# Two transformer blocks on one core: compression and gates with high and low parts side by side, and value stages that take the token halves in turn

## What is computed

```python
def compress(z, pe, w1, w2):
    zb = z[:, blk] + pe[None, None, :, None, :]
    zb = zb.transpose(0, 1, 3, 2, 4).reshape(b, n_cmp, NSA_KV_HEADS, CMP_LEN * HEAD_DIM)
    return jax.nn.silu(zb @ w1) @ w2
k_cmp = compress(k_c, cmp_pe[0], cmp_w1[0], cmp_w2[0])
v_cmp = compress(v_c, cmp_pe[1], cmp_w1[1], cmp_w2[1])
...
gates = jax.nn.sigmoid(gl.reshape(b, s, NSA_HEADS, 3))
```

## Time and profile before

| | |
|---|---|
| median of 3 runs | 2095.44 us (2095.3 to 2095.66) |
| the profiled execution | 2095.29 us |
| its span | 2093.5 us |
| TensorE busy | 2056.4 us, 98% |
| VectorE busy | 1482.3 us, 71% |
| ScalarE busy | 1022.6 us, 49% |
| GpSimd busy | 483.1 us, 23% |
| mean granted TensorE clock | 0.996 |
| DMA | 369.99 MB, 177 GB/s |

### The profile page before, as it was taken

How to read it: one execution, slowest core, us unless ns; L and a number is a source line. 1 busy time by engine, 2 the same in 40 slices (tenths; PEclk the granted TensorE clock), 3 DMA queues, 4 the chain that set the end, 5 groups by cost and what they waited for, 6 DMA issues and landing times.

```text
span 2093.5 us, 29532 instructions
## 1 busy us (share of the span) xinstructions
PE 2056.4 (98%) x11608; PEld 1771.4 (85%) x11608; DVE 1482.3 (71%) x2054; ACT 1022.6 (49%) x1508; POOL 483.1 (23%) x441
## 2 busy tenths in 40 slices
PE   7999999999999999999999999999999999999997
PEld 6788888888888888887878888888888888888886
DVE  8866778788776556876646668777776567777755
ACT  5445444455633554653455555554544344455443
POOL 8305553300000344340211224310110001101122
PEclk9999999999999999999999999999999999999999
DMA  7554566556654333555444445555556665655664
GB/s 249 172 185 155 178 191 194 190 184 221 218 185 149 121 109 118 181 203 186 161 150 146 143 151 181 182 191 183 191 190 181 189 191 185 191 187 186 186 186 131
DMA packets 104090, 369.99 MB, mean 177 GB/s; under 512 B 11632, under 2 KB 12944, under 8 KB 103824
## 3 DMA queue, kind: packets, MB, share of 16 engines
q1 hardware_dynamic: 103952, 368.11, 55.6%
HBM read 365.97 MB, written 2.10 MB: 176 GB/s over the span
## 4 chain that ended last, share of the span: by engine, by line
PE 94%; DVE 4%; issue 0%; ACT 0%; DMA 0%; DVEq 0%; SPq 0%; ACTq 0%
PE psg L511 51%; PE psg L513 25%; PE psg L558 2%; PE psg L560 2%; PE psg L559 2%; PE psg L510 2%; DVE s_wl L1579 2%; PE pst L511 1%; PE pst L595 1%; DVE s_rh L1597 1%; PE pst L513 1%; DVE s_ry L1597 1%; PE pss L759 1%; PE pso L779 0%; PE pst L683 0%; PE pst L684 0%
## 5 line engine op out<-in xcount | busy, mean ns | idle before, releaser
L1579 DVE TENSOR_TENSOR s_wl<-s_stage,s_wh 128x1024 fp32r<-128x1024 f32 (+3 forms) x699 | 871.5, 1247 | 374.5 <-ACT s_wh L1050 371.6
L1050 ACT ACTIVATE s_wh<-s_stage 128x1024 fp32r<-128x1024 f32 (+3 forms) x699 | 729.1, 1043 | 789.9 <-PE psg L511 429.0
L511 PE MATMUL psg<-s_ry,s_wh 128*128 128x512 f32 x2672 | 941.0, 397 | 3.3 <-DVE s_mv L1646 2.5
L513 PE MATMUL psg<-s_ry,s_wl 128*128 128x256 f32 x2501 | 706.8, 283 | 0.0
L511 PEld LDWEIGHTS psg<-s_ry,s_wh 128*128 128x128 f32 x2672 | 492.5, 188 | 111.4 <-issue 3.1
L513 PEld LDWEIGHTS psg<-s_ry,s_wl 128*128 128x128 f32 x2501 | 470.6, 188 | 7.7
L511 PE MATMUL psg<-s_rh,s_wh 128*128 128x512 f32 x1280 | 456.9, 400 | 10.9 <-DVE s_rh L1597 9.1
L513 PE MATMUL psg<-s_rh,s_wl 128*128 128x256 f32 x1180 | 334.7, 284 | 0.0
L511 PEld LDWEIGHTS psg<-s_rh,s_wh 128*128 128x128 f32 x1280 | 237.4, 189 | 61.1 <-issue 8.0
L511 PE MATMUL psg<-s_hid,s_wh 128*128 128x512 f32 x704 | 244.6, 394 | 0.0
L513 PEld LDWEIGHTS psg<-s_rh,s_wl 128*128 128x128 f32 x1180 | 223.8, 190 | 3.6
(11 more groups left out here) (390 smaller groups left out, 2280.1 us busy)
## 6 DMA issues: line engine op xcount, KB each, us to landing
...
```

The source lines that it names most:

```text
L511: m = e.matmul(o, M.WH[:, r, ws], xx, start=begin, stop=end)
L513: m = e.matmul(o[:, T:2 * T], M.WL[:, r, ws], xh, start=False, stop=False)
L1050: e.activation(M.WH[:, c % NR, 0:n], M.ST[:, c % NS, 0:n], ACT.Copy).then_inc(S["wh"], 1)
L1579: e.tensor_tensor(M.WL[:, c % NR, 0:n], M.ST[:, c % NS, 0:n], M.WH[:, c % NR, 0:n], ALU.subtract).then_inc(S["wl"], 1)
```

## The change

*Side by side.* The z parts now lie in one [128, 128] tile, high part in columns 0 to 59 and low part in 64 to 123, and `WH` and `WL` are two views of one tile `W` [128, 3, 2, 1024]. One matmul of 512 columns (256 of the high and 256 of the low part of w1) replaces three of 256; the product low x low is computed along with them. The accumulator is then a whole bank: VectorE sums its two halves (`hsum`), and a real matmul with a 0/1 matrix `stk` adds the rows of the high and the low part while it turns them over; it replaces the transposes, and tanh and silu come behind it on 128 columns. The gate's unit is stored so that its high and low 36 columns stand side by side, sixteen matmuls with 72 outputs replace sixteen pairs, and a matmul with `gstk` adds and turns over.

*Spread.* The row of units becomes

```diff
@@ -61,6 +61,8 @@
...
     put("ident", (p == f).astype(np.float32))
+    put("stk", (p % 64 == f[:, 0:64]).astype(np.float32))
+    put("gstk", ((p < 72) & (p % 36 == f[:, 0:36])).astype(np.float32))
@@ -236,7 +238,7 @@
...
         for w in range(2):
-            for _ in range(3):
+            for _ in range(3 if w == 0 else 0):
@@ -244,13 +246,13 @@
...
                 yield
-            for _ in range(4):
+                if w == 0 and m < 5:
+                    yield
+            for _ in range(6):
...
             yield
-            if w == 0:
-                yield
@@ -283,9 +285,9 @@
...
     P.group([(("kc", j), P.halves("wkv", j)) for j in range(4)])
+    P.between = P.compress()
...
         P.tile(("vc", j), P.halves("wkv", 4 + j))
-    P.between = P.compress()
@@ -345,8 +347,8 @@
...
         self.ST = fix("stage", [128, NS, UW])
-        self.WH = fix("wh", [128, NR, UW], F32R)
-        self.WL = fix("wl", [128, NR, UW], F32R)
+        self.W = fix("w", [128, NR, 2, UW], F32R)
+        self.WH, self.WL = self.W[:, :, 0, :], self.W[:, :, 1, :]
@@ -462,7 +464,25 @@
...
 
-        return self.ZB[m % 3][:, part, i, :].rearrange("p (h n) -> p h n", h=4)[:, :, 0:15]
+        return self.ZB[m % 3][:, i, 64 * part:64 * part + 64].rearrange("p (h n) -> p h n", h=4)[:, :, 0:15]
+
+    def gate_weights(self, r):
+
+        return self.W[:, r, :, :].rearrange("p s c -> p (s c)")[:, 0:KT * 72].rearrange("p (k c) -> p k c", k=KT)
+
+    def weights(self, c, part, n):
+
+        if n == KT * 36:
+            return self.gate_weights(c % NR)[:, :, 36 * part:36 * part + 36]
+        return self.W[:, c % NR, part, 0:n]
+
+    def staged(self, c, n):
+        s = self.ST[:, c % NS, 0:n]
+        return s.rearrange("p (k c) -> p k c", k=KT) if n == KT * 36 else s
+
+    def hid(self, part):
+
+        return self.HT[:, part, :, :].rearrange("p a (h n) -> p a h n", h=4)[:, :, :, 0:16]
@@ -541,15 +561,15 @@
...
         banks = [P.bank[t, i] for i in range(2)]
-        vacant(*banks)
-        for i in range(2):
-            held[banks[i]] = P.out[t, i]
+        vacant(banks[0])
...
             w.wait_ge("wl", c + 1)
-            steps = [(kk, i) for i in range(2) for kk in range(2)] if u == 7 else [(kk, i) for kk in range(2) for i in range(2)]
+            steps = [(kk, i) for i in range(2) for kk in range(2)] if u in (0, 7) else [(kk, i) for kk in range(2) for i in range(2)]
             for n, (kk, i) in enumerate(steps):
+                if u == 0 and n == 2:
+                    vacant(banks[1])
@@ -562,6 +582,8 @@
...
             unit()
+        for i in range(2):
+            held[banks[i]] = P.out[t, i]
@@ -679,22 +701,22 @@
...
                     ws = slice(i * 256, i * 256 + 256)
-                    o = M.PST[:, 0, 0:T]
-                    e.matmul(o, zb[:, 0, i, :], M.WH[:, r, ws], start=(m == 0 and i == 0), stop=False)
-                    e.matmul(o, zb[:, 0, i, :], M.WL[:, r, ws], start=False, stop=False)
-                    x = e.matmul(o, zb[:, 1, i, :], M.WH[:, r, ws], start=False, stop=(m == 7 and i == 3))
+                    x = e.matmul(M.PST[:, 0, :], zb[:, i, :], M.W[:, r, :, ws], start=(m == 0 and i == 0), stop=(m == 7 and i == 3))
...
                 yield
-            held["t", 0] = ("hcs", v + 1)
-            for _ in range(3):
+                if v == 0 and m < 5:
+                    yield
+            held["t", 0] = ("hsum", v + 1)
+            yield
+            vacant(("s", 0))
+            w.wait_ge("hsum", v + 1)
+            for k in range(2):
+                x = e.matmul(M.PSS[:, 0, 64 * k:64 * k + 64], M.ZT[v][:, 128 * k:128 * k + 128], M.con("stk", 64), start=True, stop=True)
+            x.then_inc(S["hct"], 1)
+            held["s", 0] = ("hcs", v + 1)
+            for _ in range(5):
                 yield
-            vacant(("s", 0))
-            w.wait_ge("hcs", v + 1)
-            e.transpose(M.PSS[:, 0, 0:128], M.ZT[v][:, 0:128], ident)
-            e.transpose(M.PSS[:, 0, 128:256], M.ZT[v][:, 128:256], ident).then_inc(S["hct"], 1)
-            held["s", 0] = ("htl", v + 1)
-            yield
@@ -713,16 +735,28 @@
...
             held["o", 0] = ("cmp", v + 1)
-            if v == 0:
-                yield
-                yield
+            yield
+
+    def gate_tile():
+
+        bank = P.bank["gate"]
+        vacant(bank)
+        held[bank] = P.out["gate"]
+        c = done[0]
+        r = c % NR
+        w.wait_ge("wl", c + 1)
+        for k in range(KT):
+            ready("h1")(k)
+            m = e.matmul(M.product(bank)[0:72, :], M.gate_weights(r)[:, k, :], Y(k)[1], start=(k == 0), stop=(k == KT - 1))
+        m.then_inc(S["units"], 1)
+        unit()
...
         for t in range(2):
-            m = e.transpose(M.PSO[1][:, 36 * t:36 * t + 36], M.ZT[0][0:36, t * 128:t * 128 + 128], ident[0:36, 0:36])
+            m = e.matmul(M.PSO[1][:, 36 * t:36 * t + 36], M.ZT[0][0:72, t * 128:t * 128 + 128], M.con("gstk", 36, 72), start=True, stop=True)
@@ -1047,7 +1081,7 @@
...
             w.wait_ge("units", c - NR + 1)
-        e.activation(M.WH[:, c % NR, 0:n], M.ST[:, c % NS, 0:n], ACT.Copy).then_inc(S["wh"], 1)
+        e.activation(M.weights(c, 0, n), M.staged(c, n), ACT.Copy).then_inc(S["wh"], 1)
@@ -1199,42 +1233,51 @@
...
-            w.wait_ge("units", P.end["cw1", v])
...
+            w.wait_ge("hct", v + 1)
...
-            e.activation(M.ET[v][:, :], M.PST[:, 0, 0:T], ACT.Tanh, scale=0.5).then_inc(S["hct_a"], 1)
...
-            w.wait_ge("hct", v + 1)
-            e.activation(M.HT[:, 0, :, :], M.PSS[:, 0, 0:T].rearrange("p (a b) -> p a b", a=2), ACT.Copy).then_inc(S["hth"], 1)
+            e.activation(M.ET[v][:, 0:128], M.PSS[:, 0, 0:128], ACT.Tanh, scale=0.5).then_inc(S["hct_a"], 1)
...
+            w.wait_ge("hcs", v + 1)
...
+            e.activation(M.hid(0), M.ET[v][:, 128:256].rearrange("p (a h n) -> p a h n", a=2, h=4), ACT.Copy).then_inc(S["hth"], 1)
@@ -1856,48 +1899,54 @@
...
+            w.wait_ge("units", P.end["cw1", v])
...
+            e.tensor_reduce(M.ZT[v][:, :], M.PST[:, 0, :].rearrange("p (s t) -> p t s", s=2), AX.X, ALU.add).then_inc(S["hsum"], 1)
...
-            he, bank = M.ET[v][:, :], M.PST[:, 0, 0:T]
+            he, hs = M.ET[v][:, 0:128], M.ET[v][:, 128:256]
...
-            e.tensor_tensor(M.ZT[v][:, :], bank, he, ALU.mult).then_inc(S["hcs"], 1)
+            e.tensor_tensor(hs, M.PSS[:, 0, 0:128], he, ALU.mult).then_inc(S["hcs"], 1)
...
-            e.tensor_tensor(M.HT[:, 1, :, :], M.PSS[:, 0, 0:T].rearrange("p (a b) -> p a b", a=2), M.HT[:, 0, :, :].bitcast(F32),
...
+            e.tensor_tensor(M.hid(1), hs.rearrange("p (a h n) -> p a h n", a=2, h=4), M.hid(0).bitcast(F32), ALU.subtract).then_inc(S["htl"], 1)
...
+                side.start(later(1, rope(3, M.KCMP[0:32, :, 0:15], M.COS[:, 31:256:16], M.SIN[:, 31:256:16], 4, 15, M.RTC, ("cmp", 1))))
@@ -1459,11 +1502,11 @@
...
     side.start(kv_norm())
-    nxt(5)
...
     side.start(h1_high(0, 8))
+    nxt(5)
+    side.start(compress())
     nxt(8)
-    side.start(compress())
@@ -2114,14 +2163,14 @@
...
     side.start(kv_norm())
+    side.start(h1_low(0, 8))
...
         nxt()
-    side.start(h1_low(0, 8))
+    side.start(compress())
     tiles("vc", 4, M.VC, None, 0)
-    side.start(compress())
@@ -2469,10 +2518,11 @@
...
     ticks(8)
-    ticks(8)
...
     for i in range(3):
-        e.memset(M.ZB[i][:, :, :, :].bitcast(F32), 0.0).then_inc(S["zz"], 1)
+        e.memset(M.ZB[i][:, :, :].bitcast(F32), 0.0).then_inc(S["zz"], 1)
+    e.memset(M.HT[:, :, :, :].bitcast(F32), 0.0).then_inc(S["zz"], 1)
+    ticks(8)
```

More of the change, by code:

```diff
@@ L36 @@
 _off = 0
-for _n, _w in (("ident", 128), ("cm", 128), ("ca", 32), ("c01", 32), ("ipool", 64),
+for _n, _w in (("ident", 128), ("stk", 64), ("gstk", 36), ("cm", 128), ("ca", 32), ("c01", 32), ("ipool", 64),
                ("inv", 1), ("sgn", 1)):
@@ L414, in __init__ @@
         self.VC = alloc(l1c, "vc", [128, 4, T])
-        self.ZB = [alloc(l1c, f"zb{i}", [128, 2, 4, 128], F32R) for i in range(3)]
+        self.ZB = [alloc(l1c, f"zb{i}", [128, 4, 128], F32R) for i in range(3)]
         self.HT = alloc(l1c, "ht", [128, 2, 2, 128], F32R)
@@ L670, in compress @@
         for v in range(2):
-            for _ in range(3):
+            for _ in range(3 if v == 0 else 0):
                 yield
@@ L974, in tensor_program @@
     side.start(gates())
-    tile("gate", Y, ready("h1"), (16,), 0, 36)
+    gate_tile()
     for j in range(4):
@@ L1201, in compress, with zb @@
     def compress():
-        for v in range(2):
-            def zb(m):
-                Z = (M.KC, M.VC)[v]
-                w.wait_ge("zz", 3)
-                w.wait_ge(*P.out[("kc", "vc")[v], 3])
-                if m >= 3:
-                    w.wait_ge("units", P.zb[8 * v + m - 3])
-                elif v:
-                    w.wait_ge("units", P.zb[7])
-                for i in range(4):
-                    l = 4 * m + i
```

(62 more changed lines are left out.)

33 lines of the change are left out of this document (16 added, 17 removed).

## The result

The change takes the kernel from 2095.85 us to **2088.7 us** (medians of six runs each, 2087.18 to 2090.98 after): ratio 0.9965, 95% interval 0.9956 to 0.9975. That is 7.2 us where 11.5 were forecast (2083.8). It lies inside the stated range, 0.3 us from its upper end.

The account below looks back on a forecast made before the run. PE (TensorE) was taken as the bound, busy 2056.4 of 2093.5 us, with DVE right behind in the compression's stage. Terms summed to -11.5, so 2095.3 - 11.5 = 2083.8 us; range 2080.5 to 2089.0.

Parts of the forecast that it names:

- rival A: Stage `vs` becomes bound by DVE and loads: +6.0 and more replaces +3.1, 2086.7 up to 2090; chance 0.15.
- compression, first matrix: Per compression unit, four 512-column matmuls replace twelve of 256, 1.44 us becoming 0.93; over 16 units -8.2 us.
- gate tile: Sixteen 512-column matmuls replace sixteen pairs, so sixteen matmuls of 0.120 us go: -1.9 us.
- `stk`, `gstk` for transposes: Sums over high and low rows: six real fp32 matmuls with a 0/1 matrix replace six transposes, +0.6 us.
- `vcc`, `vb`, `va`: Value stages where PE no longer waits for both accumulators, or waits less between halves: -1.3, -1.3 and -0.7 us.
- `vs`, end of the compression, new seams, DVE's lead: Wait gone at `vs` -1.1, last compression step moved inside `vw` -1.5, two new seams +0.8, DVE falling behind +3.1.
- Value stages: First accumulator takes six matmuls before the second is needed: -1.3 `vcc`, -1.3 `vb`, -1.1 `vs`; -0.7 between `va` halves.
- What the shorter units cost: Where short and long units alternate in `vs`, DVE falls back 4.4 us and PE waits for it: +3.1 us.
- The new seams behind `vs` and `vw`: `vs` now borders on `vw`, and `vw` on the q tiles: +0.8 us for the two, 0 to 1.5.
- Rival B: Nothing is lost to shorter units, since ACT and DVE run further ahead than counted: 2080.7 us; chance 0.07.
- Rival D: Slower: shifted addresses slow PE's reads in every tile, 6 ns on each of 4656 matmuls, +28 us: 2112; chance 0.03.
- POOL's zeroing and the rows of `h1`: Zeroing moves ahead of its eight ticks, the rows into the `kc` group, both beside idle engines: zero.

Follow-up runs that it names:

- after_aligned: The changed kernel with 28 more unused columns of constants, so the normed rows start again at a multiple of 512 bytes; 2084.76 us, ratio 0.9946 to the kernel before.
- experiment 8: after_aligned with the first matrix's eight units one to one with the vc and ks units, not after every second one; 2083.31 us, ratio 0.9945.

## Why the prediction was right, and what it missed

Direction and range held; the forecast itself was 4.9 us too low. The range reaches as far as 2089.0 for the sake of rival A, which did not come; that it also covers what the layout costs is luck. By its steps, measured in after_aligned against before, where the layout is out of the way:

| step | predicted | measured |
|---|---|---|
| compression, first matrix | -8.2 | -8.0 (16 units of 1.43 us, now of 0.93) |
| gate tile | -1.9 | -1.8 |
| `stk`, `gstk` for transposes | +0.6 | +0.4 for the four `stk` (0.36 us a matrix by starts, where two transposes took 0.14 to 0.22); the two `gstk` are in the row above |
| `vcc`, `vb`, `va` | -1.3, -1.3, -0.7 | -1.4, -1.4, -0.7 |
| `vs`, end of the compression, new seams, DVE's lead | -1.1 - 1.5 + 0.8 + 3.1 = +1.3 | +1.9 (what is left of the 5.7 us won between `kc` and the q tiles) |
| all further stages, as far as the clock is the same | 0 | 0.0; in the change itself some +4 |
| sum | -11.5 | -11.0 (medians of after_aligned and before: -11.2) |

The profiled execution of after_aligned itself is only 9.2 us shorter than that of before. It has 0.3 us more in the first 75 us, and 1.5 more behind the score matmuls, where its clock is at the lower level twice as long (6.8 us against 3.4).

*Compression and gate.* Right within 0.2. The moving tile of two runs kept the pace of one, as read from the tiles. The rule of the Trainium skill would have made the gains smaller (TensorE: Matmul & The Clock Gate, Back-to-back issue gap: columns over 2.4 GHz plus 2.5 ns). Here a 512-column matmul of the new units starts every 0.2325 us (0.93 for four), 8% above its 0.216, and the rows were the better guide.

*Value stages.* Right: undoing them costs what their terms add up to. `vb` gives 1.4 in after_aligned but 1.0 in the change, since PE reaches the attention's transposes 0.5 us ahead of GpSimd there (the wait for `s_csc`).

*What the shorter units cost.* The size was right: by PE's starts some 3 us of waits and restarts more than before, against 3.1. The new seams behind `vs` and `vw` were put too low: 0.8 and 0.6, 1.4 us with their restarts, where I had 0.8. The reasoning was right only in part, and that the size came out is partly luck. The count behind it takes 5.5 us for seven rotation pieces, where 0.60 each makes 4.2, so by its own rows DVE falls back by 3.1 us and not by 4.4. PE did wait in `vs`, where rotation pieces and alternation meet. But experiment 8 shows that alternation costs nothing in `vc` and `ks`, so the credit that I gave the spread of the first matrix, and denied rival A for, was for nothing. Rival A did not come: no wait in `vs` is over 0.7 us. Rival B neither. I left out that a stop also delays the matmul behind the restarted one by some 0.1 us (514.21 to the next start in the change: 0.34 in place of 0.23).

*Rival D is the one that acted, at a smaller price.* I gave it 0.03 and computed 6 ns on each of 4656 matmuls, 28 us. The change paid about 2 ns on each pair in the FFN (3.49 us over some 1700 pairs) and less elsewhere, 4 us in all. Two things in its treatment were wrong. First, I named two causes together, the weights in one tile and the shift of the addresses behind, and argued against both with one row. That row, compares tensors that lie at the same place within 256 bytes, so it could say nothing about another place. Second, I treated it as all or nothing ("from 2.5 ns each on, the change loses") and left it out of the sum, where no row spoke against a nanosecond or two. The step that failed is the argument against D, "three tensors at three places now have the same pace within that", and with it the cost of the layout, which the sum puts at nothing and which measured 4 us.

*POOL's zeroing and the rows of `h1`.* PE's starts show no loss from them: its distance to the kernel before stays at 0.3 us from 74 us to the `vc` tiles. Zero was right.
